# Dilated scores in two passes over 128 rows, and gate projections moved between the second pair's rope projections

## The reference

```
x = x + 0.5 * swiglu(rmsnorm(x), w1_a, w3_a, w2_a)            # D_FF 2816
h = rmsnorm(x)
q_sb, k_sb, v_sb, q_dl, k_dl, v_dl, gate_pre = split(h @ w_in)
g_sb, g_dl = sigmoid(gate_pre + b_gate)                       # 1024 channels each
y_sb = stick_breaking(q_sb, k_sb, v_sb) @ w_sb_out            # 8 heads of 64
y_dl = dilated(rope(q_dl), rope(k_dl), v_dl) @ w_dil_out      # 3 groups x 4 kv heads of 64
x = x + (g_sb * y_sb + g_dl * y_dl) @ w_o
x = x + 0.5 * swiglu(rmsnorm(x), w1_b, w3_b, w2_b)
return rmsnorm(x)
```

## Time and profile before

| what | value |
|---|---|
| median of three runs | 1127.63 us (1126.98 to 1127.87) |
| the profiled execution, device time | 1127.22 us |
| its span in the trace | 1125.3 us |
| mean granted TensorE clock | 0.997 |
| PE busy | 1101.4 us, 98% |
| DVE busy | 770.2 us, 68% |
| ACT busy | 543.7 us, 48% |
| PE's share of the chain that ended last | 85% |

### The profile page before, as it was taken

The page is one execution under the profiler, slowest core; times in us unless marked ns, Lnnn a source line. Parts: engine busy times, 40 slices in busy tenths (PEclk is TensorE's granted clock), DMA queues, the critical chain, the costliest instruction groups (busy, mean ns, idle before and its releaser), DMA issues.

```text
span 1125.3 us, 15594 instructions
## 1 busy us (share of the span) xinstructions
PE 1101.4 (98%) x6033; PEld 943.5 (84%) x6033; DVE 770.2 (68%) x1090; ACT 543.7 (48%) x870; POOL 2.7 (0%) x6
## 2 busy tenths in 40 slices
PE   8999999999999999999999999999999999999996
PEld 6888899988998788877777778788898899889985
DVE  7876378745868778678765556667774578637864
ACT  6554155523644456567755543425552355415642
POOL 0000000000000000000000000000000000000000
PEclk9999999999999999999999999999999999999999
DMA  8323233332324212111112113422233323333222
GB/s 295 96 75 113 75 113 113 113 94 94 93 73 131 79 39 75 56 38 53 51 57 75 52 57 96 142 94 94 90 104 106 95 94 113 94 94 113 82 68 75
DMA packets 34295, 103.18 MB, mean 92 GB/s; under 512 B 4144, under 2 KB 7472, under 8 KB 34224
## 3 DMA queue, kind: packets, MB, share of 16 engines
q1 hardware_dynamic: 34224, 102.21, 28.9%
HBM read 100.10 MB, written 2.10 MB: 91 GB/s over the span
## 4 chain that ended last, share of the span: by engine, by line
PE 85%; DVE 6%; ACT 4%; issue 3%; SPq 1%; DMA 1%; POOL 0%; POOLq 0%; DVEq 0%; ACTq 0%
PE acc_pair L1208 24%; PE acc_pair L1209 24%; PE acc_pair L1210 24%; PE pair_bank L1208 2%; PE pair_bank L1210 2%; PE pair_bank L1209 2%; DVE w_lo L785 1%; PE bank L1208 1%; PE bank L1210 1%; PE bank L1209 1%; ACT rope L646 1%; ACT w_hi L487 1%; DMA w_raw<-in_w13a 1%; PE bank L1216 1%; PE bank L1218 1%
## 5 line engine op out<-in xcount | busy, mean ns | idle before, releaser
L1208 PE MATMUL acc_pair<-xg_hi,w_hi 128*128 128x512 f32 (+1 forms) x693 | 265.5, 383 | 1.5 <-DVE w_lo L1016 1.5
L1209 PE MATMUL acc_pair<-xg_lo,w_hi 128*128 128x512 f32 (+1 forms) x693 | 259.8, 375 | 0.0
L1210 PE MATMUL acc_pair<-xg_hi,w_lo 128*128 128x512 f32 (+1 forms) x693 | 259.1, 374 | 0.0
L487 ACT ACTIVATE w_hi<-w_raw 128x1024 fp32r<-128x1024 f32 (+3 forms) x159 | 154.3, 976 | 147.9 <-PE acc_pair L1210 147.3
L785 DVE TENSOR_TENSOR w_lo<-w_raw,w_hi 128x1024 fp32r<-128x1024 f32 (+3 forms) x159 | 178.6, 1126 | 42.3 <-ACT w_hi L487 41.3
L1210 PEld LDWEIGHTS acc_pair<-xg_hi,w_lo 128*128 128x128 f32 x693 | 130.5, 188 | 24.6
L1208 PEld LDWEIGHTS acc_pair<-xg_hi,w_hi 128*128 128x128 f32 x693 | 130.8, 189 | 23.1 <-issue 2.8
L1209 PEld LDWEIGHTS acc_pair<-xg_lo,w_hi 128*128 128x128 f32 x693 | 131.0, 189 | 19.9 <-issue 0.7
L1210 PE MATMUL acc_pair<-hid_hi,w_lo 128*128 128x512 f32 x352 | 138.8, 394 | 0.0
L1209 PE MATMUL acc_pair<-hid_lo,w_hi 128*128 128x512 f32 x352 | 138.2, 393 | 0.0
L1208 PE MATMUL acc_pair<-hid_hi,w_hi 128*128 128x512 f32 x352 | 136.9, 389 | 0.0
(11 more groups left out here) (220 smaller groups left out, 2059.7 us busy)
## 6 DMA issues: line engine op xcount, KB each, us to landing
w_raw<-in_w13b SPq DMA_DIRECT2D x44, 512.0 KB, 3.6
w_raw<-in_w13a SPq DMA_DIRECT2D x40, 512.0 KB, 3.8
w_raw<-in_wmix SPq DMA_DIRECT2D x22, 512.0 KB, 3.5
w_raw<-in_w2a SPq DMA_DIRECT2D x16, 512.0 KB, 3.6
w_raw<-in_w2b SPq DMA_DIRECT2D x16, 512.0 KB, 3.5
w_raw<-in_wgate SPq DMA_DIRECT2D x8, 512.0 KB, 3.5
w_raw<-in_wend SPq DMA_DIRECT2D x8, 512.0 KB, 3.5
w_raw<-in_wo SPq DMA_DIRECT2D x8, 512.0 KB, 3.5
```

The lines of the kernel that those rows point to most:

```text
L487: act.activation(w_hi[:, s, 0:width], w_raw[:, s, 0:width], ACT.Copy).then_inc(whi_done, 1)
L1208: pe.matmul(o, w_h, r_h, start=first, stop=False, skip_group_check=check)
L1209: pe.matmul(o, w_h, r_l, start=False, stop=False, skip_group_check=check)
L1210: return pe.matmul(o, w_l, r_h, start=False, stop=last, skip_group_check=check)
```

## The change

Three things change.

**Dilated scores.** The two heads of a pair lie in partitions 0 to 63 and 64 to 127. Before, a product used 64 partitions and three passes. After, for each head the hi half of q stands in its own 64 partitions and the lo half in the other 64; the key's hi half stands in both (two DMAs of 64 partitions copy it across, `twin_done`), and the key's lo half stands in its own partitions with zeros in the others (written by POOL, `zeros_done`). Two passes over 128 rows then give hi·hi + lo·hi and hi·lo. ACT and DVE write hi and lo of a rope projection in two instructions of 64 partitions each, in place of one of 128.

**Order.** The first fill takes 5 half units in place of 4. Gates 0, 1 and 2 of the first attention stand between the second pair's rope projections, the sb output units follow later, one gate of the second attention (gdl 0) moves into the list, and the third entry of `DL_FILL` is 3.

**Room.** Five of the eight gate tiles lie in the buffers that rope used (rope2, roped, cos, sin). The END loop is written out, with each gdl unit one place ahead of its dil unit; it ends gdl 7, dil 6, dil 7.

```diff
-             + [("rk", 1, 0)] + [("rq", 1, g) for g in range(NG)] + [("rv", 1, 0)])
+MIX_ORDER = (PROJ[0:FIRST] + [PROJ[FIRST], ("gate", 0, 0), PROJ[FIRST + 1], ("gate", 1, 0), PROJ[FIRST + 2],
+                             PROJ[FIRST + 3], ("gate", 2, 0), PROJ[FIRST + 4], ("sb", 0, 0)]
+             + [u for m in range(EARLY_GATES, KD) for u in (("gate", m, 0), ("sb", m - EARLY_GATES + 1, 0))]
+             + [("gdl", 0, 0), ("sb", 6, 0), ("sb", 7, 0)])
+END_ORDER = [u for m in range(KD - 1) for u in (("gdl", m + 1), ("dil", m))] + [("dil", KD - 1)]
...
-DL_FILL = (2,) * 16
+DL_FILL = (2, 2, 3) + (2,) * 13
...
-    fill(4)
+    fill(SB_FIRST)
...
+                if ("suffix", 2 * SB_PAIRS - 1) in s:
+                    tanh()
...
+                if u - 7 in KEYS:
+                    sp.wait_ge(op_hi_done, split_parts(nth(u - 7) + 1))
+                    for head in (0, 1):
+                        key = stacked(u - 7, head).bitcast(F32)
+                        sp.dma_start(key[head_rows(head + 1), :], key[head_rows(head), :]).then_inc(twin_done, 16)
...
+                        for head in (0, 1):
+                            rows = head_rows(head)
+                            act.activation(stacked(w, head)[rows, :], src[rows, :], ACT.Copy).then_inc(op_hi_done, 1)
...
+                    pool.memset(dk_lo[jp][head_rows(head + 1), head, :].bitcast(F32), 0.0).then_inc(zeros_done, 1)
...
-                        dve.tensor_tensor(lo, roped[:], hi.bitcast(F32), ALU.subtract).then_inc(op_lo_done, 1)
+                        for head in (0, 1):
+                            rows, hi = head_rows(head), stacked(w, head)
+                            lo = hi[head_rows(head + 1), :] if what == "rq" else dk_lo[pair][rows, head, :]
+                            dve.tensor_tensor(lo, roped[rows, :], hi[rows, :].bitcast(F32),
+                                              ALU.subtract).then_inc(op_lo_done, 1)
...
-                    product(bank[0], dq_hi[jp][rows, 0, own], dq_lo[jp][rows, 0, own], dk_hi[jp][rows, :],
-                            dk_lo[jp][rows, :], True, False, True)
-                    for g in (1, 2):
-                        mm = product(bank[1][:, (g - 1) * P:g * P], dq_hi[jp][rows, g, own], dq_lo[jp][rows, g, own],
-                                     dk_hi[jp][rows, own], dk_lo[jp][rows, own], g == 1, g == 2, True)
+                    for g in range(NG):
+                        o = bank[1][:, (g - 1) * P:g * P] if g else bank[0]
+                        keys = own if g else slice(0, SEQ)
+                        pe.matmul(o, dq2[jp][:, a, g, own], dk2[jp][:, a, keys], start=g < 2, stop=False,
+                                  skip_group_check=True)
+                        mm = pe.matmul(o, dq2[jp][:, a, g, own], dk_lo[jp][:, a, keys], start=False, stop=g != 1,
+                                       skip_group_check=True)
```

More of the change, by code:

```diff
@@ L75 @@
 OUT_POOL = (0, 1)
-GATE_COLS = ((0, 1024), (1024, 512))
-END_COLS = ((0, 1024), (1024, 256))
+GATE_COLS = {"gate": slice(0, 1024), "sb": slice(1024, 1536)}
+END_COLS = {"gdl": slice(0, 1024), "dil": slice(1024, 1280)}
 SB_BANKS = (((1, 0), (3, 384)), ((2, 0),), ((0, 0),))
@@ L84, in chunk_base, with unit_kind, is_proj @@
     return base + sum(2 * n + KD for _, n in CHUNKS[:c])
+def unit_kind(u):
+    return MIX_ORDER[u - MIX] if u < END else END_ORDER[u - END]
+def is_proj(u):
+    return MIX <= u < END and unit_kind(u) in PROJ
 def unit_width(u):
@@ L93, in unit_width @@
                 return n * P
[L94 to L97 removed]
+    if MIX <= u < WO:
+        return {"sb": SB_PAIRS * P, "dil": DL_PAIRS * P}.get(unit_kind(u)[0], KD * P)
     return KD * P
@@ L113, in mix_schedule, with tanh @@
     halves = [(half, u) for u in range(MIX, END)
-              for half in (("Us",) if u >= GATE and (u - GATE) % 2 else ("Ua", "Ub"))]
+              for half in (("Us",) if unit_kind(u)[0] == "sb" else ("Ua", "Ub"))]
+    tanhs = []
+    def tanh():
+        while tanhs:
+            s.append(("tanh", tanhs.pop(0)))
     def fill(n):
@@ L174, in mix_kind, with nth, split_parts @@
     return MIX_ORDER[u - MIX]
+def nth(u):
+    return PROJ.index(mix_kind(u))
 def through(*units):
-    return max(MIX_ORDER.index(u) for u in units) + 1
+    return max(PROJ.index(u) for u in units) + 1
+def split_parts(n):
+    return sum(2 if what in ("rq", "rk") else 1 for what, _, _ in PROJ[:n])
+KEYS = [u for u in FINS if mix_kind(u)[0] == "rk"]
 ROPES = [u for u in FINS if mix_kind(u)[0] in ("rq", "rk")]
@@ L378, in gsb, with gate_at @@
         def gsb(m):
-            return gsb_tiles[:, KD - 1 - m, :]
+            if m < EARLY_GATES:
+                return gsb_tiles[:, m, :]
+            return (rope2[:, 0, :], rope2[:, 1, :], roped[:], cos[:], sin[:])[m - EARLY_GATES]
+        def gate_at(u):
+            what, m = unit_kind(u)[0:2]
+            if what == "gate":
+                return gsb(m)
+            return gd_tiles[:, m, :] if m < EARLY_DL else gdl[:, m % 2, :]
         def wait_lo(engine, u0, i):
@@ L387, in head_rows, with stacked @@
             return slice(HD * (h % 2), HD * (h % 2) + HD)
+        def stacked(w, head):
+            what, pair, g = mix_kind(w)
+            return dq2[pair][:, head, g, :] if what == "rq" else dk2[pair][:, head, :]
         def v_parts(t):
@@ L399, in reads @@
         def reads(u0, i):
-            n = len([u for u in range(u0 % RING, u0, RING) if not MIX <= u < GATE])
+            n = len([u for u in range(u0 % RING, u0, RING) if not is_proj(u)])
             return n + i
@@ L1225, in bank_free @@
                     return
-                if not MIX <= last < GATE:
+                if not is_proj(last):
                     pe.wait_ge(acc_read[u0 % RING], reads(u0, i))
@@ L1462, in _ @@
                     mm.then_inc(pv_done, 1)
-            with pe.Fori(0, KD // 4) as i:
-                for j in range(0, 8, 2):
-                    unit(END + j, 2 * i, xg, K8)
-                    if j == 0:
+            for u in range(END, WO):
+                what, m = unit_kind(u)
+                if what == "gdl":
+                    unit(u, 0, xg, K8)
+                else:
+                    if m == 0:
                         pe.wait_ge(ys_done, 2 * (SB_PAIRS + DL_PAIRS))
-                    unit(END + j + 1, 2 * i, yd, K8[0:DL_PAIRS])
+                    unit(u, 0, yd, K8[0:DL_PAIRS])
             for m in range(KD):
@@ L1537 @@
     first = {"q": 0, "k": SBT, "v": 2 * SBT, "rq": 3 * SBT, "rk": 3 * SBT + DQT, "rv": 3 * SBT + DQT + DL_PAIRS}
-    order = [first[what] + DL_PAIRS * g + pair for what, pair, g in MIX_ORDER]
+    order = [first[what] + DL_PAIRS * g + pair for what, pair, g in PROJ]
     gate0 = first["rv"] + DL_PAIRS
```

202 lines of the change are left out of this document (106 added, 96 removed).

## The result

The changed kernel takes 1149.21 us (median of 5 runs, 1147.64 to 1149.38), the kernel before 1126.98 us beside it (1126.39 to 1127.87): a ratio of 1.019, 95% interval 1.0179 to 1.0201. It is slower, as forecast, but by 20.5 us in the profiled executions (spans 1125.3 and 1145.8) where 5.8 were forecast. 1149 us lies outside the stated range of 1120 to 1141.

What follows compares the result with a forecast made beforehand. PE was taken to set the time nearly everywhere, if ACT and DVE stay ahead. The terms −2.6 + 2.55 + 4.3 + 4.6 − 7.3 + 2.75 + 1.5 gave +5.8 us: 1133.0 profiled, 1133.3 predicted, 8-in-10 range 1120 to 1141.

Steps and rivals of the forecast that it cites:

- Step 7: PE's clock: half clock after long waits, mostly covered by the next wait; +1.5 us, bounds 0 and +5.
- U to the first transposes: From the last first-pair query projection's end (U) to block 0's transposes: 54.0 us against 49.7, +4.3 us.
- step 4: From U to the end of the rope projections: ACT and DVE chains make PE wait; +4.3 and +4.6 us.
- Step 1: Dilated scores in two passes over 128 rows: 0.91 us gained a block, counted for eight blocks, −7.3 us.
- Step 2: First fill of 5: the wait before the first scores and its half-clock stretch go; −2.6 us.
- step 3: Heads 4 to 6 of the first attention: shifted steps and dearer rope splits delay scores 5 and pv 4; +2.55 us.
- 5: END into WO: first weight split waits for a gate's tanh, last two merges stand in a row; +2.75 us.
- 6: The rest: SP's wait and DMAs ahead of a weight load, POOL's zeros, half units moved from END; 0.
- Step 4b: First transposes to block 6's: ACT and DVE chains set the time, 58.6 us against 54.0, +4.6 us.
- Rival A: Faster: DVE and ACT interleave better, PE leads through the rope projections too; 1109 us, half of it 1122; chance 0.22.
- Rival C: Slower still: half clock in the bare places and longer chains, +5 us, 1138 us; chance 0.18.

Runs made afterwards that it cites:

- e4: Changed kernel with idle matmuls, result never read, put into PE's long waits; 1141.03 us, ratio 1.0124.
- e17: As e4, with more of PE's waits filled with idle matmuls, those at WO too; 1140.65 us.
- e2: Changed kernel with its dilated scores in three passes on 64 rows again, new order kept; 1155.79 us.
- e7: Changed kernel with the three gates behind the last v projection, no longer between the second pair's projections; 1148.26 us, ratio 1.0195.
- e5: Changed kernel with a first fill of 4 half units in place of 5; 1141.56 us, ratio 1.0121.
- e6: Two passes in the old order, but with a first fill of 5 half units; 1150.59 us, ratio 1.0198.
- e12: As e6, with the roped projection's last steps behind the block's sum and scale in the first four dilated blocks; 1140.22 us.
- e14: Changed kernel with roped projections' last steps, gate and tanh behind the block's sum and scale in the first four dilated blocks; 1149.16 us.
- e8: Two passes in the old order, each roped projection split by one hi and one lo instruction of 128 partitions, scores wrong; 1119.41 us, ratio 0.9931.
- e18: Changed kernel with one hi and one lo instruction of 128 partitions per roped projection, dilated scores wrong; 1132.68 us, ratio 1.0062.
- e9: Two passes in the old order with first fill of 4, idle matmuls put into PE's waits; 1132.09 us.
- e16: Two passes in the old order, 128-partition splits copied into the stacks by DMA, idle matmuls added in the waits; 1120.93 us.

## Why the prediction was wrong

**Step 7 failed, the term for the clock.** It stood at +1.5 us with a bound of +5. The trace has 18.5 us of PE work lost to half clock in place of 1.7, and taking PE's idleness away (e4, e17) gives 8.2 to 8.6 us of time back. That is some 7 of the 14.7 us missed (7.2 between the profiled executions of the changed kernel and e17). The term's reason was that the next wait would cover the work lost. That holds only for part: the chain of ACT and DVE starts, in every block, from scores and half units that PE delivers, so a slow PE also delays the chain. By its own segments, U to the first transposes took 59.6 us (forecast 54.0, in e17 with the clock full 55.2), block 0 to block 6 612.93 − 551.42 = 61.5 (forecast 58.6, in e17 59.2). So the chain lengths of step 4 were right to about a microsecond each at full clock. Block by block the forecast's 10.1, 13.3, 8.1, 9.1, 10.5 and 7.5 us were 10.3, 13.5, 8.0, 9.4, 10.6 and 7.4 in e17: that agreement is too close for luck. The Trainium skill, TensorE: Matmul & The Clock Gate, section What's actually happening, says that the throttled clock is the default and activity lifts it. e4 and e17 agree with that: with the waits filled, e17 has the full clock from 480 to 620 us. The forecast had leant on the two waits of 1.6 us that were not followed by half clock, and on cover by the next wait, for waits of 2.2 to 3.8 us.

**The rest of the miss**, about 7 of 14.7 us, is spread and only in part explained. In e17, with the clock full, U came at 490.5 where the forecast's own terms give 488.3 (491.03 − 2.7 for suffix 5 − 2.6 + 2.55): 2.2 us late. pv of head 2 waited 0.75 us that was not foreseen, and the wait before scores 5 was 0.8 longer than forecast. Step 4 was 1.8 us longer. Step 1's gain was 0.80 us a block, not 0.91, which is 8 × 0.11 = 0.9 us in the sum (the short matmuls and the first one behind them cost 0.11 more). At the end of the kernel half clock lasted 11.6 us (11.1 in e17) where before it lasted 6.1; in the traces its length there varies by several microseconds between kernels with the same end. How much of these is chance I can't say.

**Steps that held.** 2: no wait and no half clock before the first scores. 3: scores 5 2.6 us late (forecast 1.8). 4: waits of 2.3, 1.3, 1.2 and 3.1 us against 1.8, 2.1, 1.3 and 3.5. 5: 1.15 and 2.06 us against 1.1 and 2.25. 6: nothing. e2 bears out that only eight blocks profit.

**Reasons that fell though the number held.** Step 4b blamed the gates between the rope projections for separate round trips; e7 without them takes as long, so the number came out right for this order and would have been nearly as high without the gates (58.8 us in e7, from block 0 to block 6). The half unit's shift counts for 7.7 us (e5). In the old order much of its cost is the place of the fins in the queues (e6, e12), in the changed one the cost lies ahead of the dilated blocks, and its cause there stays open (e14). Step 2 booked that same half unit as a gain of 2.6 us. And step 3 booked the doubled parts as 5 us on each engine, "none of it on PE", and let them enter only inside the chains. Put by themselves (e8, e18), the doubled parts are the dearest part of the change that these runs separate, 12.5 to 16.5 us with the clock that follows, more than the 8.6 us that two passes are worth without them. Rival A (the waits go) had as its test under 50 us from block 0 to block 6; it was 61.5. Rival C had the right mechanism, with a price of 5 us that was too small by 11.

## What to carry to other kernels

Where two engines hand work to and fro and PE leads by less than a microsecond a block, work added to the hand-over can count in full, even on engines that are idle a third of the time: here 11 us of it cost 12.5. Price it first, by itself, before the gain on PE. A list whose steps are shifted by half a unit changes what stands ahead of each step in the queues of ACT and DVE: look at that order, step by step, before moving the first fill. And when a change adds waits of PE, price the clock behind them as well: here filling the waits gave 8.2 us back, while in e9 and e16, where the chain took the gain back, it gave nothing.
